# Weight pieces that begin 0, 64 or 128 bytes further on, by projection

## What is computed

```python
def reference(x, ...):
    x = first_block(x, ...)     # mixer + attention, gated MLP with a causal convolution, gated embedding
    return second_block(x, ...) # 2 layers: sparse / latent attention, memory attention, mixture of 16 experts

# first_block
proj = rms_norm(x) @ w_in                       # 1024 -> 2048: u, q, k, v
y = concat(pool_mixer(u), attention(q, k, v)) @ w_out
gate, val = split(rms_norm(x) @ w_up, 2)        # 1024 -> 5632
x = x + rms_norm((gelu(conv(gate)) * val) @ w_down)
x = x + (p @ w_ple) * sigmoid(x @ w_ple_gate)
# second_block, layer 0: nsa_w_in (1024 -> 2596), attention, w_out; layer 1: mla_w_in (1024 -> 672), attention, w_out
# each layer ends in hier_moe: 2 of 4 experts of one of 4 groups per token
```

## Time and profile before

| | before |
|---|---|
| median of 3 runs (lowest, highest) | 1030.02 us (1029.99, 1031.07) |
| the profiled execution's own time | 1034.57 us |
| its span, first to last instruction | 1032.7 us |
| mean granted TensorE clock | 0.994 |
| TensorE matmuls busy | 987.7 us, 96% |
| VectorE, ScalarE, GpSimd busy | 54%, 39%, 10% |
| matmuls of L1035 | 2496 of 5874 |

### The profile page before, as it was taken

The page is one execution under the profiler, slowest core; times in us unless marked ns, Lnnn a source line. Parts: engine busy times, 40 slices in busy tenths (PEclk is TensorE's granted clock), DMA queues, the critical chain, the costliest instruction groups (busy, mean ns, idle before and its releaser), DMA issues.

```text
span 1032.7 us, 15441 instructions
## 1 busy us (share of the span) xinstructions
PE 987.7 (96%) x5874; PEld 675.7 (65%) x5874; DVE 556.7 (54%) x1209; ACT 402.7 (39%) x793; POOL 107.5 (10%) x141
## 2 busy tenths in 40 slices
PE   7999999999999999899999999989999999999984
PEld 7977899999886889777633434338677734334332
DVE  5765656666446754775423433457675513434364
ACT  5465456555435545683312112123474312121110
POOL 0721001111001100151001000000132001000000
PEclk9999999999999999999999999999999999999997
DMA  9872576645545453808999999996357999999992
GB/s 328 205 250 88 190 244 205 203 164 177 191 164 198 143 173 105 324 3 357 397 423 421 410 421 420 421 396 234 115 243 302 394 418 421 411 421 420 422 406 94
DMA packets 96110, 292.31 MB, mean 283 GB/s; under 512 B 11086, under 2 KB 48126, under 8 KB 72478
## 3 DMA queue, kind: packets, MB, share of 16 engines
q1 hardware_dynamic: 96030, 291.24, 74.1%
HBM read 289.98 MB, written 1.25 MB: 282 GB/s over the span
## 4 chain that ended last, share of the span: by engine, by line
PE 79%; DVE 8%; DMA 6%; ACT 3%; issue 2%; POOL 1%; SPq 0%; DVEq 0%; POOLq 0%; ACTq 0%
PE ps L1035 36%; PE ps L1488 16%; PE ps L1526 9%; DMA arena<-in_moe_w_up 3%; DMA w<-in_moe_w_up 3%; DVE yTr L2383 2%; PE ps L1141 2%; PE ps L1171 2%; PE ps L1152 2%; PE ps L977 2%; PE ps L1463 1%; PE ps L1536 1%; PE ps L1336 1%; DVE plo L1748 1%; PE ps L984 1%
## 5 line engine op out<-in xcount | busy, mean ns | idle before, releaser
L1748 DVE TENSOR_TENSOR plo<-w,phi 128x1024 fp32r<-128x1024 f32 (+3 forms) x147 | 177.4, 1226 | 135.0 <-ACT phi L2564 134.9
L2564 ACT CAST phi<-w 128x1024 fp32r<-128x1024 f32 (+3 forms) x147 | 148.5, 1032 | 139.0 <-PE ps L1035 131.8
L2383 DVE SCALAR_TENSOR_TENSOR yTr<-ps,small,yTr 32x512 fp32r<-32x512 f32 x112 | 83.7, 748 | 181.0 <-ACT yTr L2861 179.4
L1488 PE MATMUL ps<-w,arena 128*64 128x512 f32 x464 | 135.6, 594 | 1.3 <-DMA w<-in_moe_w_up 1.3
L1035 PE MATMUL ps<-hTr,phi 128*128 128x256 f32 x472 | 133.1, 282 | 0.0
L1035 PE MATMUL ps<-hTr,plo 128*128 128x256 f32 x472 | 132.5, 281 | 0.0
L1035 PE MATMUL ps<-yTr,phi 128*128 128x256 f32 x472 | 132.5, 281 | 0.0
L1035 PE MATMUL ps<-phi,hTr 128*128 128x512 f32 (+2 forms) x240 | 93.9, 391 | 0.8 <-issue 0.7
L1035 PE MATMUL ps<-phi,yTr 128*128 128x512 f32 (+2 forms) x240 | 93.5, 389 | 0.7 <-DVE hTr L1740 0.7
L1035 PEld LDWEIGHTS ps<-yTr,phi 128*128 128x128 f32 x472 | 90.2, 191 | 0.0
L1035 PEld LDWEIGHTS ps<-hTr,phi 128*128 128x128 f32 x472 | 88.8, 188 | 0.2
(11 more groups left out here) (362 smaller groups left out, 1732.8 us busy)
## 6 DMA issues: line engine op xcount, KB each, us to landing
w<-in_moe_w_down SPq DMA_DIRECT2D x31, 1024.0 KB, 18.8
w<-in_moe_w_up SPq DMA_DIRECT2D x31, 1024.0 KB, 18.2
w<-in_moe_w_gate SPq DMA_DIRECT2D x27, 1024.0 KB, 15.8
w<-in_w_up SPq DMA_DIRECT2D x22, 1024.0 KB, 7.6
arena<-in_moe_w_up SPq DMA_DIRECT2D x19, 1024.0 KB, 16.2
arena<-in_moe_w_gate SPq DMA_DIRECT2D x15, 1024.0 KB, 20.8
arena<-in_moe_w_down SPq DMA_DIRECT2D x13, 1024.0 KB, 21.0
w<-in_w_out SPq DMA_DIRECT2D x6, 2048.0 KB, 10.2
```

What stands on the lines that cost most here:

```text
L1488: ins_ = e.matmul(bank[64 * ee:64 * ee + 64, :], xg[:, k, o:o + 64], half_view(i, kind, p, ee, ab)[:, c, :], start=(k == 0), stop=(k == 7))
L1748: e.tensor_tensor(plo[:, 0:m], slots[u % 3][:, j * m:j * m + m], phi[:, 0:m].bitcast(F32), ALU.subtract).then_inc(s_cut)
L2383: ins_ = e.scalar_tensor_tensor(y_parts[t][other, part], psum[2 + hf][own_, :], slot_gate[own_, p:p + 1], y_parts[t][own_, part].bitcast(F ...
L2564: e.copy(pieces[p % 4][0][:, 0:m], slots[u % 3][:, j * m:j * m + m]).then_inc(s_cast)
```

## The change

Pieces are put 0, 16 or 32 words (0, 64 or 128 bytes) further on, by a table of units: `in0` and `up0` to `up3` stay; `in1`, `up4` to `up7`, `oa0` and `oa1` move by 64 bytes; all others move by 128 bytes. `plo` moves with its `phi`. The 128 bytes that the last place then needs are taken from `line_gap` (48 words to 16) and put behind the pieces, so `x` moves by 128 bytes too, and everything behind it stays. Since a shifted piece reaches into the place behind it, `cast` waits for the latest earlier piece whose words overlap its own (`over`) in place of piece p - 4, and SyncE's waits before it loads into `w3` and `w4` are made to fit.

```diff
+SHIFTS = dict(in0=0, in1=16, oa0=16, oa1=16, **{f"up{u}": u // 4 * 16 for u in range(NJ // 2)})
...
-                with ExitStack() as same:
-                    pieces = [[same.enter_context(nc.sbuf_tensor(f"{n}{j}", [128, 1024], F32R))
-                               for n in ("phi", "plo")] for j in range(4)]
+                pieces = {}
+                for shift in (0, 16, 32):
+                    with ExitStack() as same:
+                        if shift:
+                            same.enter_context(nc.sbuf_tensor(f"shift{shift}", [128, shift], F32R))
+                        pieces[shift] = [[same.enter_context(nc.sbuf_tensor(f"{n}{j}_{shift}", [128, 1024], F32R))
+                                          for n in ("phi", "plo")] for j in range(4)]
             slots.append(sb(f"w{i}", [128, 4096]))
+        sb("piece_gap", [128, 32])
         x = sb("x", [128, 2, D])
-        sb("line_gap", [128, 48])
+        sb("line_gap", [128, 16])
...
                 piece.append((u, j, m))
+                shift_of.append(SHIFTS.get(name, 32))
...
+        def piece_place(p):
+            return pieces[shift_of[p]][p % 4]
+
+        def words(p):
+            return p % 4 * 2048 + shift_of[p], p % 4 * 2048 + shift_of[p] + 2048
+
+        def over(p):
+
+            return max((q for q in range(max(p - 7, 0), p) if words(q)[0] < words(p)[1] and words(p)[0] < words(q)[1]),
+                       default=None)
...
-                        e.wait_ge(s_pc, 2 * (done - (done - 1 - (n - 14)) % 4))
+                        e.wait_ge(s_pc, 2 * max(done - (done - 1 - k) % 4 for k in range(max(n - 15, 0), n - 13)))
...
-                    if p >= 4:
-                        e.wait_ge(s_pc, 2 * (p - 4) + 2)
-                    e.copy(pieces[p % 4][0][:, 0:m], slots[u % 3][:, j * m:j * m + m]).then_inc(s_cast)
+                    if over(p) is not None:
+                        e.wait_ge(s_pc, 2 * over(p) + 2)
+                    e.copy(piece_place(p)[0][:, 0:m], slots[u % 3][:, j * m:j * m + m]).then_inc(s_cast)
```

More of the change, by code:

```diff
@@ L421, in build @@
         w_m, w_kv, w_o2 = ins["mla_w_in_2"][0], ins["mem_w_kv_2"], ins["w_out_2"]
-        units, piece, name_of = [], [], {}
+        units, piece, shift_of, name_of = [], [], [], {}
         def unit(name, parts, m=0, n=0):
@@ L1039, in cut @@
                 e.wait_ge(s_cut, p + 1)
-                return [a[:, 0:piece[p][2]] for a in pieces[p % 4]]
+                return [a[:, 0:piece[p][2]] for a in piece_place(p)]
             def tok3_steps(bks, pair, n, p0, steps, each=2, rows=None, ready=None):
@@ L1745, in cut @@
                     u, j, m = piece[p]
-                    phi, plo = pieces[p % 4]
+                    phi, plo = piece_place(p)
                     e.wait_ge(s_cast, p + 1)
```

## The result

The change is slower: 1050.12 us (median of 4 runs, 1046.89 to 1051.76) beside 1030.01 us (median of 4, 1029.99 to 1031.07) for the kernel before, a ratio of 1.0185 with a 95% interval of [1.0169, 1.0202]. The forecast was 1036.5 us, its range 1031 to 1041: the direction was right, the size was not. The profiled execution of the change took 1051.76 us, that of before 1034.57 us; the two profiles differ by 17.2 us, the two medians by 20.1 us. The sum further down takes the second difference apart. All four executions of the kernel before, beside which the ratio was taken, lie near 1030 us; e1 shows that this kernel has a second time near 1034.8 us, and beside that the change is some 15 us slower.

A forecast was written before the change was run, and what follows sets the result against it. TensorE was taken to bound the kernel, its matmuls busy for 987.7 of 1032.7 us. Wait +8.4, clock +1.2, pace -1.8 and -1.3 gave +6.5 us, put on the median of 1030.0: 1036.5 us, range 1031 to 1041.

The forecast's parts named there:

- terms 1 and 2: Pace of matmuls reading shifted pieces, moving and stationary: 1.8 us and 1.3 us gained.
- term 3: The casts' new waits for later pieces: 8.4 us lost on TensorE, all from one cast.
- the thirteenth cast: Cast of piece 123, first of `oa0`, now waits for `n5`: attention of layer 0 begins 8.4 us later.
- the other twelve: Casts at in0/in1, in1/in2, up3/up4, up7/up8 wait one piece, 2.8 us, later; covered by 5.6 us, cost nothing.
- term 4: Clock at 1.2 GHz when layer 0's attention begins, after TensorE's gaps: 1.2 us lost; bounds none and 3.2 us.
- term 1: Matmuls with pieces moving: 888 shifted by 128 bytes gain 2 ns each, 1.8 us; bounds 2.9 us gained or lost.
- the new offsets collide more: Rival: 2.9 + 3.9 us lost in pace, up to 1046.4 us, with half of it 1043 us; chance 0.10.
- Term 2: Matmuls with pieces stationary: a third of 864 moved ones draw the fast pace, 1.3 us gained; bounds 3.9 us either way.
- I take none: Experts of layer 0: of the delay at the attention at most 1.9 us could be given back; none was counted.
- The offset does nothing to the pace: Rival: the pace gains are nothing, only wait and clock count, 1039.6 us; chance 0.22.

The follow-up runs named there:

- e1: The kernel before, run again unchanged: four executions from 1029.91 to 1030.85 us, six from 1034.23 to 1035.48; ratio 1.0007.
- e2: The kernel before with only the cast of piece 123 made to wait for `n5`'s piece, no address moved: 1043.74 us, ratio 1.0093.
- e4: e2 with 11 and 7 small unused matmuls that keep TensorE busy in the two gaps: 1039.3 us, ratio 1.0076.
- e5: The change with `in0` to `in2` and up back at offset 0, the rest, `oa` included, at 128 bytes: 1037.59 us, ratio 1.0037.
- e7: Scan in one kernel: units put at different offsets from 0 to 192 bytes, read by unit; two executions, 1041.24 and 1041.81 us.
- e3: The change with `oa0` and `oa1` at 128 bytes, so the cast of 123 waits for 119 again: 1039.75 us, ratio 1.0071.
- e9: e8 with the moving pieces (in3, out, dn, pg, n, oa) and n5 at 192 bytes, other units at 0: 1031.86 us, ratio 1.0013.
- e12: e9 with all units ahead of up at offset 0 too: 1029.39 us, ratio 0.9982.
- e8: The kernel before with 2 in place of 6 keep-busy matmuls ahead of up, leaving a short gap: 1029.77 us, ratio 0.9952.

## Why the prediction was wrong

By its own steps, in us between the two profiles:

| step | predicted | measured | from |
|---|---|---|---|
| terms 1 and 2, pace | -3.1 | +3.5 | 0.35 in up, 2.2 in dn to n3, 0.3 in `oa`, 0.65 ahead of up (1.2 less the wait of 0.54) |
| ahead of `in0` | 0 | +0.6 | the table of stages; not the change's |
| term 3, the thirteenth cast | +8.4 | +8.1 | `n5` to the attention; e2, e4: 8.0 |
| term 3, the other twelve | 0 | +0.54 | the wait ahead of the first attention |
| term 4, clock | +1.2 | +2.6 | attention to `oa0`; e4: 0.0 with TensorE kept busy |
| on the way to the end (experts of layer 0) | 0 | +1.9 | `oa`'s end to `m0` |
| **sum** | **+6.5** | **+17.2** | |

**The step that failed first is term 1.** "With 512 columns I take 2 ns" less: it was 4.5 ns more. The evidence was the earlier trace rows, two halves of a piece of 416 columns. Of that shape it was true: by the starts in the trace of before the first half runs at 191 ns and the second, 128 bytes further modulo 256, at 187; in the change the halves swap, 187 and 191, and `m0` as a whole keeps its 189. With 512 columns the same 128 bytes work the other way round, 228.8 to 233.3 ns. The prediction named this ("the row is from one shape only") as the bound and forecast by the row all the same; and the bound, 2.9 us lost, was a little narrow (the 888 less the 96 of `m0` and n4, whose pace did not change, are 792, and 792 x 4.5 ns is 3.6 us, of which the 0.4 of `ob` does not reach the end). Term 1 turned round is half of what the rival "the new offsets collide more" said, at 0.10; e5 and e7 show that half. The other half, a step of 4.5 ns down in term 2, did not come: beside the long pace of the profile before, up4 to up7 lost 0.8 ns and up8 to up10 nothing.

**Term 2** had the two paces right and the draw wrong. I counted on a third of the moved units drawing the short pace at the new offset. At 64 bytes there is only 118.6, at 128 bytes 117.8 in every profile, with or without the gap. The units that had 113.3 ns at offset 0 and moved (n5, m1) lost it. The counts of both terms, like the section on which operand the pieces are, leave out the 96 matmuls of `mk0`, with pieces stationary, and `mv0`, with 256 columns of a piece moving. They move by 128 bytes too, and from the first of them to `out0` it is 22.9 us in both traces, so nothing rests on it.

**The sum was put on the wrong base.** The difference of 6.5 us was taken against a profiled execution with the long pace in up and added to a median of executions that had the short one. The 4.5 us between the two were seen and not asked after, although held the answer: 1056 matmuls x 4.5 ns is 4.7 us. In the change only up0 to up3 can still draw the short pace, so a kernel at 1030 is compared with one that has lost most of that chance. This is why the medians differ by more than the profiles: 20.1 = 17.2 + 4.5 (the profile of before above its median) - 1.6 (the profile of the change above its own). Nor can a difference of 0.2% be told from no change in a kernel whose two times lie 4.7 us apart. What spreads the change's own executions over 4.9 us is not shown. Their mean clocks are 0.988 in the two longest, 0.990 and 0.992 in the shortest, which would be worth 0.004 x 1048 = 4.2 us, an estimate.

**Term 3** held: the waits are 5.9 and 2.1 us where 5.9 and 3.9 were named, and 8.1 for 8.4 us in all; e3 takes the wait away and gives 10.4 us back, clock included. Of the other twelve "they cost nothing" is true for the casts and wrong for what stands behind them. In the trace of before ScalarE casts the last piece of `in2` at 37.43 us and copies `q` out at 38.38; in the change the last two pieces come together:

```profile
37.43 1.05 ACT L2564 CAST phi<-w 128x1024 fp32r<-128x1024 f32 x1 [1.78 <-PE ps L1035]
38.38 0.59 ACT L2540 ACTIVATE arena<-ps 128x512 f32<-128x512 f32 x1
```

```profile
38.26 2.00 ACT L2582 CAST phi<-w 128x1024 fp32r<-128x1024 f32 x2 [1.80 <-PE ps L1053]
40.16 0.59 ACT L2558 ACTIVATE arena<-ps 128x512 f32<-128x512 f32 x1
```

The copy is 1.8 us later, of which TensorE's own lag explains 0.8. From there it runs through the copies, the small arithmetic and the casts of the next units to the wait that grew from 1.34 to 1.88 us; e9 makes it larger by a step of offset nearer to it, e12, without that step, has 1.4 us.

**Term 4** was right in kind and half the size: 1.2 us for what the first matmuls lose, while the clock stayed at 1.2 GHz until 445 us and the loss went on through them; the named bound of 3.2 us held. e2 shows 1.8 us for the same gaps, e4 none: in the change the clock stayed at 0.50 for the attention's first 6.1 us, in e2 for its first 4.5 us. The Trainium skill, "TensorE: Matmul & The Clock Gate", Part 1, has an idle engine fall back to 1.2 GHz, and the trace agrees: 0.50 from 431.5 us, after TensorE had been idle since 428.3.

**"I take none" given back** was right as a refusal and missed the other sign: the experts of layer 0 cost 1.9 us more than in the profile of before, 1.6 of them in the two rows on the experts' weights. The same stage is longer in e2 (1.3 us), e3 (2.0) and e4 (1.1), hardly in e5 (0.3). But it is longer in the unchanged kernel of e1 too, by 0.7 us, and by 0.9 in e8, each with 1.3 us in the row on `arena`. So up to half of the 1.9 us is what this kernel does from one execution to the next. The row of 0.9 us on `spare` is in e3 too, with 0.4 in e2, and in neither e1 nor e8. e3 has it without the delay at `n5`, so the delay alone is not its cause. What its cause is stays open.

**The rivals.** "The offset does nothing to the pace" had 0.22, and, for it, a page of the Trainium skill, "SBUF — State Buffer": TensorE never waits on anyone (section on the two separate sides), lines are of 16 bytes (Specifications). The scan speaks against what I drew from it: steps of 16 and 32 bytes split no such line and move the pace from 113.3 to 120.0 and from 228.8 to 233.3 ns. What TensorE waits for there, no run shows.

## What to carry to other kernels

When two executions of one kernel differ by several us, find the stage that differs before a difference is put on either: here it was one stage with two paces, and its size told more than the change. Read pace by the distance of starts over a whole stage, and do not carry a difference of some nanoseconds from one shape to another when it is to be multiplied by 900: its sign may turn. An offset's effect is cheap to scan, one offset for each unit in one kernel. For a wait that is moved by "only one piece", follow the in-order lists behind it to the next thing TensorE needs, for every place where it moves and not only for the largest.

## What the runs showed of the hardware

- The same 256-column matmuls at the same addresses run at 113.3 or at 117.8 ns from start to start, and keep one of the two for 120 us; in up, 43 of 88 executions had the shorter one by their time. With 512 columns the two are 228.8 and 233.3 ns (e2's `in3`). What draws it is not known: with a gap of 0.96 us ahead 31 of 42 had the shorter one, but in one of three batches its share was no larger than without.
- An offset of one operand by 16 to 192 bytes changes the pace, in up within an unbroken stream: 113.3 to 120.0 ns for stationary pieces, 226.7 to 234.3 ns for moving ones, with different best places among those tried, 0 for the one and 192 for the other; a shift of 128 bytes helps 416 moving columns (191 to 187 ns, the halves of `m0`) and costs 512 columns 4.5 ns.
- The same gaps of TensorE, 5.9 and 2.1 us, cost 2.6 us of clock in one kernel and 1.8 in another, and 0.0 where small matmuls filled them.
